# Order of the third gate and up group and the preceding expert's down products in a two-layer decoder step

## The reference, cut to what matters

```python
h = jax.nn.silu(jnp.einsum('nd,edf->nef', t, w_g)) * jnp.einsum('nd,edf->nef', t, w_u)
h = h * gate[..., None].astype(h.dtype)
return jnp.einsum('nef,efd->nd', h, w_d)
```

## Time and profile before

| what | value |
|---|---|
| median of three runs | 1887.12 us |
| lowest, highest of the three | 1884.7, 1895.98 us |
| profiled execution | 1895.87 us |
| its span, first to last instruction | 1894.2 us |
| mean granted TensorE clock | 0.902 |
| TensorE matmul busy | 1611.4 us (85%) |
| VectorE, ScalarE busy | 619.0 us, 396.3 us |
| expert stage of layer 0, of layer 1 | 646 to 952 us, 1552 to 1853 us |
| read from HBM | 366.46 MB |

### The profile page before, as it was taken

The page is one execution under the profiler, slowest core; times in us unless marked ns, Lnnn a source line. Parts: engine busy times, 40 slices in busy tenths (PEclk is TensorE's granted clock), DMA queues, the critical chain, the costliest instruction groups (busy, mean ns, idle before and its releaser), DMA issues.

```text
span 1894.2 us, 36101 instructions
## 1 busy us (share of the span) xinstructions
PE 1611.4 (85%) x15137; PEld 1036.6 (55%) x15137; DVE 619.0 (33%) x1528; ACT 396.3 (21%) x973; POOL 110.8 (6%) x186
## 2 busy tenths in 40 slices
PE   4999888888887599989935999999979759989893
PEld 2435655656565355555513766666647545555552
DVE  3231255455511211111122666676650121111112
ACT  1011254454511111000002233333320011100100
POOL 0002012112200100000020000000000010000001
PEclk9999898888998699999967999999979859999996
DMA  9265167767663399999772244444430459999973
GB/s 307 89 265 183 56 184 245 233 206 226 237 254 133 101 372 364 354 367 371 278 213 57 79 128 128 136 132 128 150 104 34 162 193 333 379 368 367 385 264 93
DMA packets 235347, 410.01 MB, mean 216 GB/s; under 512 B 16664, under 2 KB 105465, under 8 KB 235129
## 3 DMA queue, kind: packets, MB, share of 16 engines
q1 hardware_dynamic: 195808, 330.59, 50.2%
q0 software_dynamic: 14848, 48.97, 7.8%
q10 hardware_dynamic: 24524, 28.07, 5.0%
HBM read 366.46 MB, written 41.12 MB: 215 GB/s over the span
## 4 chain that ended last, share of the span: by engine, by line
PE 68%; DVE 8%; issue 5%; DMA 4%; ACT 3%; POOL 1%; ACTq 0%; SPq 0%; DVEq 0%; POOLq 0%
PE bank L1359 19%; PE bank L1853 12%; PE bank L1379 9%; PE bank L2222 4%; PE bank L770 3%; PE bank L1061 3%; PE bank L1896 2%; PE bank L1907 2%; PE bank L810 2%; PE bank L1345 1%; DMA arena<-in_state_ret 1%; PE bank L778 1%; PE bank L242 1%; PE bank L1114 1%; PE bank L1923 1%
## 5 line engine op out<-in xcount | busy, mean ns | idle before, releaser
L1359 PE MATMUL bank<-ring,arena 128*32 128x256 f32 x6144 | 367.7, 395 | 43.6 <-issue 41.9
L1359 PEld LDWEIGHTS bank<-ring,arena 128*32 128x32 f32 x6144 | 210.2, 114 | 185.1 <-issue 74.9
L1853 PE MATMUL bank<-xnT,ring 128*128 128x320 f32 x768 | 228.0, 454 | 0.9 <-ACT catT L1796 0.9
L1853 PEld LDWEIGHTS bank<-xnT,ring 128*128 128x128 f32 x768 | 150.0, 200 | 65.3 <-issue 13.0
L1379 PE MATMUL bank<-ring,arena 128*32 128x256 f32 x3072 | 171.7, 379 | 1.4 <-issue 1.4
L1480 DVE TENSOR_TENSOR arena<-arena,bank 128x128 f32<-128x128 f32 x96 | 27.7, 289 | 405.8 <-ACT arena L1424 405.8
L1379 PEld LDWEIGHTS bank<-ring,arena 128*32 128x32 f32 x3072 | 100.9, 110 | 66.1 <-issue 1.7
L770 PE MATMUL bank<-ident,ring 128*128 128x128 f32 x512 | 90.4, 325 | 28.0 <-DVE ring L946 11.5
L1424 ACT ACTIVATE arena<-bank 128x128 f32<-128x128 f32 x96 | 26.7, 278 | 409.3 <-PE bank L1359 409.3
L286 PE MATMUL bank<-ring,xnT 128*128 128x512 f32 x224 | 99.3, 604 | 6.6 <-DVE xnT L251 6.6
L770 PEld LDWEIGHTS bank<-ident,ring 128*128 128x128 f32 x512 | 65.9, 163 | 48.7 <-DVE ring L946 17.2
(11 more groups left out here) (340 smaller groups left out, 1959.8 us busy)
## 6 DMA issues: line engine op xcount, KB each, us to landing
ring<-in_w_expert_down SPq DMA_DIRECT2D x32, 2048.0 KB, 10.8
ring<-in_w_expert_gate SPq DMA_DIRECT2D x32, 2048.0 KB, 14.0
ring<-in_w_expert_up SPq DMA_DIRECT2D x32, 2048.0 KB, 19.5
ring<-in_cache_k SPq DMA_DIRECT2D x128, 256.0 KB, 3.4
ring<-in_cache_v POOLq DMA_DIRECT2D x128, 256.0 KB, 4.4
ring<-in_w_in_even SPq DMA_DIRECT2D x9, 2048.0 KB, 12.9
ring<-in_w_in_odd SPq DMA_DIRECT2D x16, 1024.0 KB, 9.4
arena<-x_slots ACTq DMA_DIRECT2D x32, 384.0 KB, 7.2
```

The lines of the kernel that those rows point to most:

```text
L1359: mm = pe.matmul(bank[2 + s][pair_rows(p), 0:256].rearrange("p (q n) -> p q n", q=2), x_in[par][:, k, 32 * s:32 * s + 32], w[:, :, k, P * ...
L1853: mm = pe.matmul(bank[c % 3][:, 0:NT], w[:, k, P * (c % 4):P * (c % 4) + P], xnT[:, k, 0:NT], start=(k == 0), stop=(k == KC - 1))
```

## The change

The third gate and up group of an expert (s = 2) stands ahead of the preceding expert's three down groups instead of behind them. The same is done on the two engines that follow: on ACT the silu of group 2 ahead of the takings and stores of y, on DVE its product ahead of the takings of y. No instruction is added or removed, SP's list is as it was.

```diff
@@ few_pe
                 if e < N_EXPERTS:
                     gate_up(e, e % 2, 1)
+                    gate_up(e, e % 2, 2)
                 if e:
                     for s in range(ST):
                         down(e - 1, 1 - e % 2, s)
-                if e < N_EXPERTS:
-                    gate_up(e, e % 2, 2)
@@ few_act
                 if e < N_EXPERTS:
                     silu(e, 1)
+                    silu(e, 2)
                 if e:
                     for s in range(ST):
                         if (ST * (E + e - 1) + s) % 2 == 0:
                             take_y(e - 1, s)
                     store_y(e - 1)
-                if e < N_EXPERTS:
-                    silu(e, 2)
@@ few_dve
                 if e < N_EXPERTS:
                     hidden(e, 1)
+                    hidden(e, 2)
                 if e:
                     for s in range(ST):
                         if (ST * (E + e - 1) + s) % 2 == 1:
                             take_y(e - 1, s)
-                if e < N_EXPERTS:
-                    hidden(e, 2)
```

## The result

The changed kernel takes 1952.48 us (median of four runs, 1951.01 to 1963.26) beside 1891.03 us for the kernel before: ratio 1.0337, 95% interval 1.0292 to 1.0382, so 61 us slower. The 1891.03 us is the median of four executions of the kernel before, the three told above and a fourth. Forecast were 1947 us and +60 us. A second measurement beside other experiments gave 1951.36 and 1890.69 us, ratio 1.0340 (1.0299 to 1.0380). The profiled execution took 1951.62 us.

What follows compares the result with a forecast made beforehand. The prediction took the expert stages to be bound by when SP issues the down piece, refilling a dry DMA queue. Its terms, 48.3+13.1-1.1 = 60.3 us on the median 1887.1, gave 1947 us, range 1916 to 1963 us.

Steps and rivals of the forecast that it cites:

- Steps 1 and 2: SP's queue: gate and up gain nothing, held behind the down piece, which is issued 3.45 us later, at their old time.
- Step 3: Expert stages: queue dry 3.45 us longer, clusters stay 23.5 us, seven landings a stage later: 2 x 7 x 3.45 = 48.3 us.
- Step 4: TensorE's clock: longer waits before odd experts slow 14 first groups by 2.05 us each, 28.7 against 15.6 today: +13.1 us.
- Step 5: End of a stage: silu and product of expert 15 hidden behind expert 14's down groups, -1.1 us for both stages.
- Step 6: ACT and DVE: no taking of y late; y stores, now in front of silu(e+1,0), cost 0.
- Step 7: SP's first weights of the next layer's mixer come 3.45 us later, into the gather of y: 0 to +3, taken as 0.
- (a): Rival on SP's queue: issued back to back, the cluster takes 20.8 us instead of 23.5; 1899 us, chance 0.10.
- (b): Rival: bytes bind, odd experts' waits spread over all, the clock's 15.6 us and ends' 1.1 won; 1870 us, chance 0.06.
- (c): Rival: nothing that can be told; the queue doesn't run dry any more, only the ends move; 1886 us, chance 0.04.
- The estimate of 28 us: Alternative for the landings: only the DMA's fixed cost of about 2 us exposed per cluster, 14 x 2 = 28 instead of 48.

Runs made afterwards that it cites:

- the control: The kernel before with only SP's loop written out for constants, same order: 1896.11 us beside 1888.38, ratio 1.0025 (0.9999 to 1.0050).

## Why the prediction was right

**What bounds it.** The reading held: the expert stages live by when SP refills a dry DMA queue. The run with only the later down piece and the one with SP's waits in TensorE's order show it from both sides.

**Steps 1 and 2** (gate and up gain nothing, the cluster starts where its tail began) are in SP's queue as forecast, down, gate and up within 1.1 to 1.4 us of each other in the rows above. From the end of an odd expert's first group to the issue of the down piece that opens the next odd cluster are 13.46 us, where before there were 10.0: the shift is 3.46 us, as forecast.

**Step 3**, 48.3 us forecast. From the start of turn 2 to that of turn 15 the stages grew by 51.8 us; 8.5 of them are slow first groups (next step), 43.3 the landings. These 43.3 are what is left when the clock is taken off, and the step had a premise that failed in part: the cluster did shrink. The six odd clusters of a stage average 23.1 us in both stages now; before they were 23.5 us in the first and 24.0 in the second, of which I had said that they were much the same. Followed along the odd experts alone, the shift of the issues gives 14 x 3.45 = 48.3 us as forecast, and the shorter clusters take 7.5 back, 2.1 in the first stage and 5.4 in the second: 40.8. The dry stretch in the stretches view is about 5 us long, as forecast.

**Step 4**, the clock, 13.1 us forecast. The fourteen first groups took 5.84, 5.24, 6.44, 5.45, 6.44, 5.31 and 5.79 us in the first stage and 4.92 to 6.39 in the second, together 28.0 us over 14 x 3.66, against 28.7 forecast; minus the 15.6 of before, +12.4. The mean of 2.05 us from two rows was luckier than it deserved to be. (The page's 8.4 us more busy time for L1359 is lower, since it counts the modelled overlap of groups that follow one another once, and more of them do now; the durations of its 96 groups one by one add up to 12.3 us more.) The waits in front are 5.9 to 6.7 us before experts 3 to 13 and 4.5 and 4.6 before the two experts 15. One thing in the 15.6 us of before was off: two of the nine slow groups before stood in front of even experts of the second stage (6 and 8), beside the odd experts' chain, and cost it about 0.5 us of their 3.1. Along the odd experts the clock thus costs +14.9 us rather than +12.4. The run with 50 transposes bears out that these microseconds count in full, or nearly.

**Step 5**, the ends, -1.1 us forecast:

```profile
964.46 5.18 PE bank L1379 x96
969.64 0.48 PE bank L1368 x3
970.12 0.70 issue
970.82 5.45 PE bank L1379 x96
```

From the end of the down groups of expert 14 to the last ones are 1.18 us, before it was 1.71: -0.53 a stage.

**Step 6**: the y stores end at 804.84 (802.87+1.97) and silu of the next group 0 runs at 805.89, when TensorE has it ready. Nothing there, as the run with TensorE's order alone confirms. **Step 7**: the gather of y in layer 0 ends with 8.51 us for its last piece, before it was 8.38: nothing.

Sum by what was measured: 43.3+12.4-1.1 = 54.6 us of the 55.75 between the profiled executions (along the odd experts 40.8+14.9-1.1, the same); the remaining 1.2 us I have not placed. The forecast was 60.3, so by these profiles it was some 5 us too high: 7.5 too high by the clusters and 1.8 too low by the clock. That the medians lie 61 us apart is in part luck: the profiled execution of before (1895.87) was one of its slower ones, and which one is taken matters. In the trace of the control (1889.97 us) turns 2 to 14 take 246.2 and 244.5 us; against it the changed kernel's grew by 58.9 us, not by 51.8. The mechanism holds in both, the last 5 us of its size lie within what executions of the kernel before differ by.

**The rivals.** (a), the queue catches up in 20.8 us: clusters of 23.1 us refute it. (b), even waits without the clock's cost, and (c), nothing: refuted by the waits of about 6 us before every second expert. The estimate of 28 us that the fixed cost of the Trainium skill ("DMA: Bandwidth & Descriptors", section "Latency and other measured facts") would have given stands against 41 to 43 us for the landings: here the dry queue counted with the whole shift of the issue, less what the clusters shrank.

## What to carry to other kernels

When work is moved on a compute engine, walk through the waits of every queue that feeds it, in their order: a queue that waits in order is held by the condition that now comes last, and the transfers behind it go out late, however early their own condition holds. Where a stage stands near the bandwidth limit, count the microseconds in which the DMA share is 0, not the mean share, and look at when the next issue ends them. And give an order change its fair trial with the feeding queue reordered too: here the same change is 3.4% slower with the old list on SP and 1.45% faster than the kernel before with the new one.

## What the runs showed of the hardware that I had not expected

Three 2 MB pieces with y and x rows beside them (odd experts 3 to 13) took 22.4 to 24.2 us from first issue to last landing in the first stage, whether the queue had been dry for 3 or for 5 us, and whether the pieces were issued over 4 us or over 1 us. The full queue moved 382 GB/s over 237 us; distances of 17.6 us between two landings, which by themselves look like a faster queue, are followed by longer ones (before: 17.6 us from 852.92 to 870.48, then 21.2). The clock's fall is not tied to one length of wait: with SP's new list a wait of 2.67 us was followed by a first group of 5.35 us at 798.56 (granted clock 0.54 in its first 3 us) and one of 2.77 us by 3.66 us at 1691.18 (1.00). In the kernel before a wait of 3.45 us cost nothing (1736.57, clock 1.00), while with 24 transposes in the wait the 3.2 to 4.0 us that were left were followed by slow groups all twelve times.
